# Start out of PSUM, PSUM operands behind the second output projection, an earlier gate for the last convolution tile, and the first row scale inside an iteration

## The reference

```python
# first block
h = rms_norm(r, g_mix);  z = h @ w_in                     # 2048 -> 10240 columns: q, k, v, gates, ...
merged = sigmoid(g_a) * y_attn + sigmoid(g_c) * y_conv
r = r + merged @ w_o
r = r + square(relu(rms_norm(r, g_mlp) @ w_up)) @ w_down
r = r + sigmoid(rms_norm(r, g_ple) @ w_ple_gate) * (p @ w_ple_proj)
# second block (16 meta tokens ahead of the 256)
u = conformer_conv(rms_norm(h, mix_pre))                  # gated projection, 31 taps, layer norm, silu, w_out
h = h + rms_norm(u, mix_post)
u = (silu(rms_norm(h, ffn_pre) @ w_gate) * (... @ w_up)) @ w_down
h = h + rms_norm(u, ffn_post)
```

## Time and profile before

| | us |
|---|---|
| median of 3 runs (2643.07 to 2645.09) | 2643.59 |
| the profiled execution | 2644.3 |
| its span, first to last instruction | 2642.3 |
| PE busy | 2560.3 (97%) |
| DVE busy | 1774.8 (67%) |
| ACT busy | 1273.2 (48%) |
| POOL busy | 443.2 (17%) |
| mean granted TensorE clock | 0.987 |

### The profile page before, as it was taken

How to read it: one execution, slowest core, us unless ns; L and a number is a source line. 1 busy time by engine, 2 the same in 40 slices (tenths; PEclk the granted TensorE clock), 3 DMA queues, 4 the chain that set the end, 5 groups by cost and what they waited for, 6 DMA issues and landing times.

```text
span 2642.3 us, 43999 instructions
## 1 busy us (share of the span) xinstructions
PE 2560.3 (97%) x14973; PEld 2263.6 (86%) x14973; DVE 1774.8 (67%) x2123; ACT 1273.2 (48%) x1603; POOL 443.2 (17%) x297
## 2 busy tenths in 40 slices
PE   6999999999999999999999999989799999999998
PEld 5888888888888888888888899978588888888887
DVE  6568776577775565665667879985866556665665
ACT  4446555554544444444445454455544444444444
POOL 3024320001100000000011267862400000000003
PEclk8999999999999999999999999999899999999999
DMA  5555546655565665655655555526356565555553
GB/s 165 167 178 172 167 144 191 191 196 187 164 191 191 190 188 189 187 190 189 187 185 178 185 154 156 159 95 200 105 189 191 192 189 187 187 191 190 186 183 116
DMA packets 497336, 465.17 MB, mean 176 GB/s; under 512 B 14411, under 2 KB 494149, under 8 KB 497221
## 3 DMA queue, kind: packets, MB, share of 16 engines
q1 hardware_dynamic: 496752, 463.92, 55.5%
q10 hardware_dynamic: 516, 0.38, 0.1%
HBM read 462.15 MB, written 2.10 MB: 176 GB/s over the span
## 4 chain that ended last, share of the span: by engine, by line
PE 89%; DVE 6%; ACT 2%; issue 2%; DMA 1%; DVEq 0%; ACTq 0%; SPq 0%
PE gp L363 52%; PE gp L365 27%; PE gp L541 2%; PE gp L542 2%; PE gp L543 2%; DVE wlo L1080 2%; PE xp L557 1%; DVE A L1129 1%; DVE A L1138 1%; DMA work<-in_conv_w_dw 1%; ACT whi L661 1%; PE xp L582 0%; DVE root L1114 0%; DVE work L1463 0%; DVE s L1091 0%
## 5 line engine op out<-in xcount | busy, mean ns | idle before, releaser
L1080 DVE TENSOR_TENSOR wlo<-stage,whi 128x1024 fp32r<-128x1024 f32 x812 | 1009.1, 1259 | 689.7 <-ACT whi L661 684.7
L363 PE MATMUL gp<-A,whi 128*128 128x512 f32 x3968 | 1398.7, 395 | 30.4 <-DVE A L1129 15.4
L661 ACT ACTIVATE whi<-stage 128x1024 fp32r<-128x1024 f32 x876 | 915.7, 1057 | 999.0 <-PE gp L365 877.8
L365 PE MATMUL gp<-A,wlo 128*128 128x256 f32 x3968 | 1117.8, 282 | 0.0
L363 PEld LDWEIGHTS gp<-A,whi 128*128 128x128 f32 x3968 | 749.8, 189 | 204.6 <-issue 22.4
L363 PE MATMUL gp<-B,whi 128*128 128x512 f32 x2496 | 873.9, 395 | 9.6 <-DVE B L1448 7.9
L365 PEld LDWEIGHTS gp<-A,wlo 128*128 128x128 f32 x3968 | 753.0, 190 | 0.4
L365 PE MATMUL gp<-B,wlo 128*128 128x256 f32 x2496 | 700.2, 281 | 0.0
L363 PEld LDWEIGHTS gp<-B,whi 128*128 128x128 f32 x2496 | 468.3, 188 | 118.3 <-issue 10.5
L365 PEld LDWEIGHTS gp<-B,wlo 128*128 128x128 f32 x2496 | 472.3, 189 | 0.1
L1569 POOL TENSOR_TENSOR sq<-r 128x512 f32 (+1 forms) x32 | 35.8, 1120 | 810.0 <-DVE r L1306 756.3
(11 more groups left out here) (257 smaller groups left out, 1258.2 us busy)
## 6 DMA issues: line engine op xcount, KB each, us to landing
stage<-in_w_in SPq DMA_DIRECT2D x160, 512.0 KB, 3.9
stage<-in_w_up SPq DMA_DIRECT2D x128, 512.0 KB, 3.7
stage<-in_w_down SPq DMA_DIRECT2D x128, 512.0 KB, 3.3
stage<-in_ffn_w_gate SPq DMA_DIRECT2D x88, 512.0 KB, 4.5
stage<-in_ffn_w_up SPq DMA_DIRECT2D x88, 512.0 KB, 4.5
stage<-in_ffn_w_down SPq DMA_DIRECT2D x88, 512.0 KB, 4.3
stage<-in_conv_w_in SPq DMA_DIRECT2D x64, 512.0 KB, 4.0
stage<-in_w_o SPq DMA_DIRECT2D x32, 512.0 KB, 4.4
```

Of the source, the lines that this page charges most:

```text
L363: nc.tensor.matmul(bank.rearrange("p (a t) -> p a t", a=2), hi, both_parts(M, kt), start=first, stop=False)
L365: done = nc.tensor.matmul(bank[:, T:2 * T], lo, M[:, kt, 0:T], start=False, stop=last)
L661: nc.scalar.activation(whi[:, slot, :], stage[:, slot, :], ACT.Copy).then_inc(hi_ready, 1)
L1080: nc.vector.tensor_tensor(wlo[:, slot, :], stage[:, slot, :], whi[:, slot, :].bitcast(F32), ALU.subtract).then_inc(lo_ready, 1)
```

## The change

It joins three changes.

- **Start.** PE transposes g_mix first, then chunks 0 and 1 of x; chunks 2 and 3 stand behind units 0 and 1 of the first panel. The chunks lie in different banks (`x_home`): xp 2-3, gp 2-3, xp 0-1, xp 2-3. ScalarE converts the weight unit ahead of each chunk, scales out of PSUM into A, and copies the chunk to r only when VectorE has made its low part (`copy_x`). VectorE takes the unit's low part ahead of the chunk's, and reads x from PSUM. The first panel no longer waits for `evacuated`. The column sums move from iteration 0 to behind the first unit of iteration 1; the row scale is made in iteration 1 behind its third unit, and the first panels' results (iteration 0) are scaled four tiles at once behind the sixth. The taps are loaded first, at unit 0 of iteration 1, the 17 vectors behind them through iterations 1 and 2, and PE transposes all of them behind iteration 3. Iterations 1 and 4 are written out, a loop covers 2 and 3.
- **Last tile of the convolution.** ScalarE takes `gates(15)` and the bias ahead of the last weight conversion of that tile. In all tiles VectorE does two taps instead of three before gating.
- **Stage post.** The row scale lies in PSUM (`post_rstd`), and so does r times the gain (`gained_r`, three banks in turn). ScalarE makes the high part of two tiles by one copy from there, and VectorE the low part by one subtraction. The squares of r go from this loop to behind units 0 to 3 of the first gated iteration, two each; that iteration's row scale is made one unit later.

The core of the diff:

```diff
+        def x_home(c):
+            return [xp[:, 2:4, :], gp[:, 2:4, :], xp[:, 0:2, :], xp[:, 2:4, :]][c].rearrange("p a (b t) -> p (a b) t", b=2)
+        post_rstd = xp[:, 1, 0:T]
+        def gained_r(h):
+            return xp[:, (0, 2, 3)[h % 3], :].rearrange("p (m t) -> p m t", m=2)
...
-                    if u == 0:
+                    if u == 0 and not (isinstance(hp, int) and hp == 0):
                         pe.wait_ge(evacuated, XSLOTS + hp - 1)
...
+            pe.wait_ge(gain_loaded, 16)
+            nc.tensor.transpose(xp[:, 1, 0:KT], first_gain, ident[0:KT, 0:KT]).then_inc(vec_turned, 1)
+            def turn_x(c):
                 pe.wait_ge(x_loaded[c], 16)
+                if c == 2:
+                    pe.wait_ge(vec_ready, 1)
+                if c == 3:
+                    pe.wait_ge(h1_ready, 4)
+                    pe.wait_ge(evacuated, 1)
...
+            turn_x(0)
+            turn_x(1)
...
-            body("qkv", 0, A, h1, {4: [lambda: column_sums(0)]})
+            body("qkv", 0, A, h1, {0: [lambda: turn_x(2)], 1: [lambda: turn_x(3)]})
+            body("qkv", 1, A, h1, {0: [lambda: column_sums(0)]})
+            with pe.Fori(2, 4) as it:
+                body("qkv", it, A, h1)
             pe.wait_ge(v_loaded, 16 * 18)
...
-            with pe.Fori(1, 5) as it:
-                body("qkv", it, A, h1)
+            body("qkv", 4, A, h1)
...
+            def hi_of_x(c):
                 act.wait_ge(x_turned, c + 1)
+                for kk in range(4):
+                    nc.scalar.activation(A[:, 4 * c + kk, 0:T], x_home(c)[:, kk, :], ACT.Copy,
+                                         scale=col("g_mix", 4 * c + kk)).then_inc(x_hi, 1)
+            def copy_x(c):
+                act.wait_ge(h1_ready, 4 * c + 4)
+                nc.scalar.activation(r[:, 4 * c:4 * c + 4, :], x_home(c), ACT.Copy).then_inc(evacuated, 1)
...
-            body("qkv", 0, root_first(0, none), {u: vectors[3 * u:3 * u + 3] for u in range(6)})
+            body("qkv", 0, none)
+            body("qkv", 1, none, {u: ([lambda: root_of(0)] if u == 2 else []) + vectors[u:u + 1] for u in range(8)})
+            body("qkv", 2, none, {u: vectors[8 + 2 * u:10 + 2 * u] for u in range(5)})
+            body("qkv", 3, none)
...
+                if i == 15:
+                    gates(15)
+                    bias_minus_centre(15)
                 hi(3)
-            gates(15)
-            bias_minus_centre(15)
...
+            for h in range(8):
+                act.wait_ge(r_updated, 48 + h + 1)
+                if h >= 3:
+                    act.wait_ge(r_ready, 48 + 2 * (h - 3) + 2)
+                for m in range(2):
+                    nc.scalar.activation(gained_r(h)[:, m, :], r[:, 2 * h + m, :], ACT.Copy,
+                                         scale=col("ffn_pre", 2 * h + m)).then_inc(post_gained, 1)
+                act.wait_ge(post_gained, 2 * h + 2)
+                nc.scalar.activation(part(A, 0, 2 * h, 2), gained_r(h), ACT.Copy).then_inc(r_hi, 2)
...
-            glu(0, 0, units={5: [lambda: root_of(6)]})
+            squares = {u: [lambda h=h: post_squares(h) for h in (2 * u, 2 * u + 1)] for u in range(4)}
+            glu(0, 0, units={**squares, 6: [lambda: root_of(6)]})
...
+            body("qkv", 0, lambda hp, it, j: add_up(hp, j, qkv_at(it, j)))
+            body("qkv", 1, qkv_tail, {2: [lambda: variance(0, 0, RMS_EPS)], 5: [scale_first]})
...
-                    taps(i - 1, REST, REST + 3, xp[:, 2 + (i - 1) % 2, :])
+                    taps(i - 1, REST, REST + 2, xp[:, 2 + (i - 1) % 2, :])
...
-                    nc.vector.tensor_tensor(u, u, by_rstd(), ALU.mult).then_inc(post_normed, 1)
-                if h >= 3:
-                    lo_of_r(24, A, "ffn_pre", h - 3)
+                    nc.vector.tensor_tensor(u, u, post_rstd.unsqueeze(1).broadcast_to([P, 2, T]), ALU.mult).then_inc(post_normed, 1)
+                if h >= 2:
+                    dve.wait_ge(r_hi, 48 + 2 * (h - 2) + 2)
+                    nc.vector.tensor_tensor(part(A, 1, 2 * (h - 2), 2), gained_r(h - 2), part(A, 0, 2 * (h - 2), 2).bitcast(F32),
+                                            ALU.subtract).then_inc(r_ready, 2)
...
-            glu(0, 0, units={5: [lambda: variance(6, 6, RMS_EPS)]})
+            glu(0, 0, units={6: [lambda: variance(6, 6, RMS_EPS)]})
```

More of the change, by code:

```diff
@@ L717, in _ @@
             act.dma_start(first_gain, io["g_mix"].rearrange("o (k p) -> (o k) p", p=P)).then_inc(gain_loaded, 16)
[L718 to L731, removed]
             act.wait_ge(vec_turned, 1)
@@ L736, in _ @@
             act.wait_ge(vec_ready, 1)
-            for c in range(4):
+            def hi_of_x(c):
                 act.wait_ge(x_turned, c + 1)
[L739 to L745, removed]
+                for kk in range(4):
[4 more added lines that the diff above has]
+                nc.scalar.activation(r[:, 4 * c:4 * c + 4, :], x_home(c), ACT.Copy).then_inc(evacuated, 1)
+            take_hi(0, 0, 0)
+            hi_of_x(0)
+            take_hi(1, 0, 1)
+            hi_of_x(1)
+            copy_x(0)
+            take_hi(2, 0, 2)
+            hi_of_x(2)
+            copy_x(1)
+            take_hi(3, 0, 3)
+            hi_of_x(3)
+            copy_x(2)
+            copy_x(3)
             def past(h):
@@ L802, in _ @@
             nc.scalar.activation(taps2[:].rearrange("p k t -> p (k t)"), xp[:, 3, 0:KT * TAPS2], ACT.Copy).then_inc(vec_ready, 1)
-            with act.Fori(1, 5) as it:
-                body("qkv", it, none)
+            body("qkv", 4, none)
             body("qkv", 5, none, {6: [norms(0)]})
@@ L1135, in _, with normed_into @@
             for c in range(4):
-                for kt in range(4 * c, 4 * c + 4):
-                    dve.wait_ge(x_hi, kt + 1)
-                    nc.vector.scalar_tensor_tensor(A[:, kt, TM:TM + T], r[:, kt, :], col("g_mix", kt),
+                take_lo(c, c)
+                for kk in range(4):
+                    kt = 4 * c + kk
+                    dve.wait_ge(x_hi, 4 * c + 2 * (kk // 2) + 2)
+                    nc.vector.scalar_tensor_tensor(A[:, kt, TM:TM + T], x_home(c)[:, kk, :], col("g_mix", kt),
                                                    A[:, kt, 0:T].bitcast(F32), ALU.mult, ALU.subtract).then_inc(h1_ready, 1)
-                take_lo(c, c)
-            def normed_into(dst, ready, first=None):
+            def normed_into(dst, ready):
                 def tail(hp, it, j):
@@ L1146, in tail @@
                     add_up(hp, j, d)
-                    if first and j == 0 and isinstance(it, int) and it == 0:
-                        first()
                     nc.vector.tensor_tensor(d, d, by_rstd(), ALU.mult).then_inc(ready, 1)
@@ L1457, in _ @@
             variance(5, 5, RMS_EPS)
-            for h in range(8 + 3):
+            for h in range(8 + 2):
                 if h < 8:
```

51 lines of the change are left out of this document (24 added, 27 removed).

## The result

| | before | after | after, measured again |
|---|---|---|---|
| median, us | 2643.33 (2641.99 to 2645.09, 4 runs) | 2616.3 (2614.32 to 2619.70, 4 runs) | 2617.0 (2615.86 to 2619.59, 4 runs) |
| ratio to before | 1 | 0.9895 [0.9883, 0.9906] | 0.9898 [0.9882, 0.9915] |
| profiled execution, us (span) | 2644.3 (2642.3) | 2614.3 (2612.5) | span 2617.8 |

A forecast was written before the change was run, and what follows sets the result against it. PE bounds the kernel, busy 2560.3 of 2642.3 us, so at most 82 us can be won in its holes. 14.3 + 8.7 - 0.8 + 0.4 = 22.6 us faster gives 2621.0 us, range 2611 to 2630.

The forecast's parts named there:

- Part 1: Taps' load moved into iteration 1, transposes behind iteration 3: PE's 11.68 us wait goes, 14.3 us won in all.
- B: Rival: taps' load starves the running weights, or the beginning stays slow; 2628 to 2632 us, chance 0.17.
- D: Rival: the taps still land as late relative to PE as before; 2635 us, chance 0.02.
- charge of 0.6 us for starved weights: Iterations 1 and 2: weights beside the taps' load come late and cost PE 0.6 us, between 0 and 8.
- Part 2: Kernel's beginning: first weight matmul at 10.35 us instead of 16.45, later a GpSimd wait of 1.2; 8.7 us won.
- bound of 11.3: Beginning, upper bound of the gain in us: unit 0 runs at full rate and GpSimd is early.
- Part 3: Behind the second output projection: second panel 9.0 us earlier, then 7.8 us wait for GpSimd; net 0.8 us lost.
- loss at the low clock: After PE's wait at the sums behind the second output projection, 7 pairs at the low rate cost 2.0 us.
- Rival A: GpSimd's additions of squares are in time, PE waits at most 2.3 us: +5 to +7, some 2614 us; chance 0.16.
- 0.1 us an instruction for PSUM operands: Behind the second output projection: possible price of VectorE reading PSUM; 16 instructions would cost 1.6 us of slack.
- Part 4: Last convolution tile: one tap less ahead of the instruction PE waits for; 0.4 us won (0 to 0.8).
- rival C: First two iterations: PE starts in bursts and stays at the low clock, 37 us lost, 2658 us; chance 0.02.

The follow-up runs named there:

- The load alone: Kernel before, with only the taps' load moved to the start of iteration 1 and PE's transposes of them behind iteration 3: 2627.96 us, ratio 0.9939.
- parts 1 and 2: Kernel before, with only the moved taps' load and the new beginning, without the post stage and last-tile edits: 2616.72 us, ratio 0.9897.
- part 3 alone: Kernel before, with only the edit of the stage behind the second output projection: 2642.14 us, ratio 0.9992.
- Short additions: Changed kernel, with GpSimd's eight additions of squares behind the second output projection only 16 of 256 tokens wide: 2605.97 us, ratio 0.9856.

## Why the prediction was right, and where it was off

**Part 1, forecast 14.3, measured 14.3 alone.** The mechanism holds in each step: idle before the transposes is zero, the load is covered, the weights beside it are slow, and PE loses little to them (rivals B and D fell). That the two numbers are equal is luck, since N moved by 1.7 us between profiles of one beginning. Two terms were mis-sized for the kernel after. The charge of 0.6 us for starved weights was zero: the units ahead covered the 10.5 us. The 18 transposes took 1.3 us (107.12 to 108.4), not 1.6. Taking N apart gives 11.68 + 2.49 - 1.3 + 2.3 = 15.2 us for this part in the kernel after. The load alone gave 0.9 less, and its trace shows most of that: the matmul at 73.40, held up for a low part, starts 0.6 us later than in an unbroken row of pairs, which is the charge of the forecast, and its first column sums stand 0.2 us later than before (41.27 for 41.09).

**Part 2, forecast 8.7, measured 10 to 11.** It begins as forecast: the first weight matmul stands at 10.43 us (10.35). N of parts 1 and 2 moved by 25.2 and the forecast's two terms are 23.0, so 2.2 us were missing, 0.9 of them in part 1. The step that was off is GpSimd's chain. I had its last addition at 43.7, it was 42.0, so the sums ended at 43.2 and not at 44.6. PE was off too, without effect: the transposes of the last two chunks of x, between matmuls at the full clock, took 1.03 us a chunk and not 1.97, and six pairs ran low, not eight. PE was thus at the sums at 40.5, not 42.5, and waited 1.56 us, not 1.2. The bound of 11.3 had named an early GpSimd as one of its reasons.

**Part 3, forecast -0.8, measured -0.4 to -1.7.** PE's start 8.5 us after the sums (8.77), the second panel 9.0 us earlier (8.7), a wait of 7.8 us (7.23), GpSimd's chain 15.9 us (15.8): each came within 0.6 us. The forecast's own sum had a slip of 0.2 there: additions from 1881.4 that take 15.9 us end at 1897.3 and not 1897.1, which makes part 3 -1.0. The loss at the low clock, 2.0 us, was 2.9 in the first profile, where the sums paid as well (sums to first pair 1.51 us for 0.67, six pairs 4.20 us for 2.1). In the second profile and with part 3 alone only two pairs ran low, 1.7 to 1.8 us in all; that difference is the one between S of 71.8 and of 70.6 and 70.5. Short additions remove the wait and give 8.8 us in S (against the second profile) and 11.0 in the median, which shows that the wait is GpSimd's. Rival A, the additions in time, would have been right with GpSimd alone on its port; it fell by the 2060 ns.

In the loop before that VectorE and GpSimd don't disturb each other, and what differs there is that one of VectorE's operands lies in PSUM. VectorE's subtraction with one operand in PSUM took 0.69 us and GpSimd's additions beside it 1.28 to 1.30, both as alone. Its conversion of weights, with both in SBUF, took 1.48 to 2.00 us beside the additions of squares (1.23 alone) and slowed them to 2.06. In the kernel after:

```profile
1845.37 1.28 POOL L1764 TENSOR_TENSOR r<-r,work 128x512 f32<-128x512 f32 x1 [0.17 <-DVE work L1499]
1845.45 0.69 DVE L1502 TENSOR_TENSOR A<-xp,A 128x512 fp32r<-128x512 f32 x1 [0.17 <-ACT A L1049]
...
1854.14 1.48 DVE L1110 TENSOR_TENSOR wlo<-stage,whi 128x1024 fp32r<-128x1024 f32 x1 [0.76 <-ACT whi L675]
1856.13 1.73 DVE L1110 TENSOR_TENSOR wlo<-stage,whi 128x1024 fp32r<-128x1024 f32 x1 [0.51 <-ACT whi L675]
```

The Trainium skill ("SBUF — State Buffer", section "Who interferes with whom") says that two SBUF inputs contend with a GpSimd instruction that reads SBUF, and one doesn't. The trace agrees in both. The 0.1 us an instruction for PSUM operands, weighed in the forecast, is in no row.

**Part 4, forecast +0.4.** The wait fell by 0.4 us; the time can't show it.

**The clock (rival C)** did not come: from 14.36 us on the pairs took 0.35 us, and 20 to 60 us ran at 1.00.

**The sum.** Read at the places it is 25.2 gained, 0.4 to 1.7 lost and 0.4 gained, 24 to 25 us, and up to 1.6 more if the one profile of the kernel before had a quick beginning (N of 171.6 for 170.1); the medians say 27.0, the two profiled spans 29.8. The forecast's 22.6 is short of the places' sum by the two steps named above, GpSimd's chain in part 2 and the small terms of part 1. The intervals of the ratios reach down to 24.8 us (first measurement), 22.5 (second) and 22.7 (parts 1 and 2 alone). In the spans, the 29.8 are 25.0 up to the projection of `p`, 1.9 from there to the last tile, 1.4 to the output projection's sums, 0.7 to the final transposes and 0.8 behind them. The 1.4 is the last tile's clock (11.02 against 9.34 us), which a second profile of the same kernel had the other way. The 0.7 holds part 3's loss of 1.7, so 2.4 us came back in a stretch of full PE that no edit touches. I take these for scatter, as the eleven profiles of the convolution show it, but whether the medians hold some of it by an effect of the change is open: no run here separates 2 us in 2600.

## What to carry to other kernels

Look at the number of rows of a small load before moving it: cutting 31 rows in 16 and 15, with the load 4 us ahead of its use, gave what putting its use 64 us behind it gave. When work is moved off one engine's path, follow the engine behind it: here the squares left ScalarE's loop and came back as a wait for GpSimd, nearly as long as what had been won. A short chain on GpSimd beside VectorE's two-operand SBUF work must be priced at its contended rate, and started as soon as GpSimd is free.

## What was not expected of the hardware

- One 248 KB load of 31 rows took 15.3 us and slowed 512 KB loads beside it from 3.5 to 14.2 us; in two loads of 16 and 15 rows it took 3.7 us, and the others 4.1.
- Transposes of 128x128 in a group of eight took 1.97 us while PE had only just begun, 1.03 between full-rate matmuls; the wait of 7 us before the sums cost another 1.7 to 2.9 us behind it, at the low clock.
- Stretches of the same instructions differed by 1.7 us in 11 us, with the granted clock at 0.88 or 1.00, from one profile of a kernel to the next. A few microseconds between two profiles are no evidence for an edit, unless they are read at its place.
